# A six-stage fp32 transformer kernel on one core: norm weights of two units applied in the split, rotary angles earlier, a shorter wait of the up units, square sums behind the first pair

## The reference, cut to what matters

```python
def sq_relu_mlp(hn, w1, w2):                  # mlp0, mlp1; w1 1024x4096, w2 4096x1024
    return jnp.square(jax.nn.relu(hn @ w1)) @ w2

# mla: h is the residual stream, normed twice with different weights
ckv = rmsnorm(h, src_g) @ w_kv_a              # 1024 x 320: 256 latent + 64 rotary columns
cq  = rmsnorm(rmsnorm(h, norm_mix_g) @ w_q_a, q_g)   # w_q_a 1024 x 384
ang = positions[..., None] * inv_freq         # rotary angles; cos(ang), sin(ang) turn k_pe and q_pe
h   = h + attention(...) @ w_o
h   = h + sq_relu_mlp(rmsnorm(h, norm_mlp_g), w1, w2)
```

## Time and profile before

| | |
|---|---|
| median of three runs | 1063.13 us |
| profiled execution | 1063.45 us, span 1061.6 us |
| PE (matmul) busy | 1005.8 us, 95% of the span |
| DVE busy | 632.8 us, 60% |
| ACT busy | 484.3 us, 46% |
| POOL busy | 62.2 us, 6% |
| chain that ended last | PE 84%, DVE 8%, ACT 4%, issue 2% |
| mean granted TensorE clock | 0.974 |

### The profile page before, as it was taken

The page is one execution under the profiler, slowest core; times in us unless marked ns, Lnnn a source line. Parts: engine busy times, 40 slices in busy tenths (PEclk is TensorE's granted clock), DMA queues, the critical chain, the costliest instruction groups (busy, mean ns, idle before and its releaser), DMA issues.

```text
span 1061.6 us, 16624 instructions
## 1 busy us (share of the span) xinstructions
PE 1005.8 (95%) x6867; PEld 934.8 (88%) x6867; DVE 632.8 (60%) x748; ACT 484.3 (46%) x619; POOL 62.2 (6%) x63
## 2 busy tenths in 40 slices
PE   7989889889999999898999999999799999999997
PEld 7988778779999999898998899999699988999996
DVE  4377654467676676667555755555765755545554
ACT  5447522156455455542444544344445644444442
POOL 1000232020000000001000000000400000000000
PEclk9989979999999999999999999999999999999999
DMA  9733400046555555353555565556446236655640
GB/s 295 200 117 120 159 1 1 1 140 222 176 196 185 174 194 160 125 166 121 185 178 179 172 197 175 186 194 191 125 137 181 93 107 218 196 187 173 195 159 40
DMA packets 128591, 165.12 MB, mean 156 GB/s; under 512 B 20862, under 2 KB 111419, under 8 KB 128411
## 3 DMA queue, kind: packets, MB, share of 16 engines
q1 hardware_dynamic: 127067, 159.57, 46.8%
q0 software_dynamic: 1312, 4.74, 1.5%
q10 hardware_dynamic: 160, 0.07, 0.0%
HBM read 163.32 MB, written 1.05 MB: 155 GB/s over the span
## 4 chain that ended last, share of the span: by engine, by line
PE 84%; DVE 8%; ACT 4%; issue 2%; POOL 1%; DMA 0%; POOLq 0%; DVEq 0%; ACTq 0%
PE ps L224 26%; PE ps L225 25%; PE ps L226 25%; DVE w_lo L205 1%; ACT w_hi L197 1%; PE ps L990 1%; PE ps L1716 1%; PE ps L1710 1%; ACT act_tmp L339 1%; PE ps L1721 1%; DVE act_lo L649 1%; PE ps L1011 1%; PE ps L891 1%; ACT act_tmp L1040 1%; DVE union L1983 0%
## 5 line engine op out<-in xcount | busy, mean ns | idle before, releaser
L205 DVE TENSOR_TENSOR w_lo<-raw,w_hi 128x2048 fp32r<-128x2048 f32 (+1 forms) x152 | 343.3, 2263 | 167.8 <-ACT w_hi L197 166.8
L224 PE MATMUL ps<-hT_hi,w_hi 128*128 128x256 f32 x1192 | 341.2, 286 | 6.0 <-ACT act_tmp L623 3.7
L225 PE MATMUL ps<-hT_hi,w_lo 128*128 128x256 f32 x1192 | 339.2, 285 | 0.0
L226 PE MATMUL ps<-hT_lo,w_hi 128*128 128x256 f32 x1192 | 339.0, 284 | 0.0
L197 ACT ACTIVATE w_hi<-raw 128x2048 fp32r<-128x2048 f32 (+1 forms) x152 | 287.1, 1891 | 101.9 <-PE ps L226 93.8
L224 PEld LDWEIGHTS ps<-hT_hi,w_hi 128*128 128x128 f32 x1192 | 230.5, 193 | 8.9 <-issue 4.5
L225 PEld LDWEIGHTS ps<-hT_hi,w_lo 128*128 128x128 f32 x1192 | 230.6, 193 | 1.7
L226 PEld LDWEIGHTS ps<-hT_lo,w_hi 128*128 128x128 f32 x1192 | 230.6, 193 | 0.0
L224 PE MATMUL ps<-w_hi,act_hi 128*128 128x512 f32 x416 | 163.9, 394 | 5.5 <-DVE act_lo L649 5.5
L225 PE MATMUL ps<-w_hi,act_lo 128*128 128x512 f32 x416 | 163.4, 393 | 0.0
L226 PE MATMUL ps<-w_lo,act_hi 128*128 128x512 f32 x416 | 162.8, 391 | 0.0
(11 more groups left out here) (289 smaller groups left out, 945.9 us busy)
## 6 DMA issues: line engine op xcount, KB each, us to landing
raw<-in_mlp_w_dram SPq DMA_DIRECT2D x64, 1024.0 KB, 5.3
raw<-in_w_up_dram SPq DMA_DIRECT2D x22, 1024.0 KB, 5.0
raw<-in_a_w_in_dram SPq DMA_DIRECT2D x16, 1024.0 KB, 5.4
raw<-in_w_in_dram SPq DMA_DIRECT2D x12, 1024.0 KB, 5.8
raw<-in_w_down_dram SPq DMA_DIRECT2D x11, 1024.0 KB, 5.0
raw<-in_a_w_out_dram SPq DMA_DIRECT2D x8, 1024.0 KB, 4.9
raw<-in_w_out_dram SPq DMA_DIRECT2D x4, 1024.0 KB, 5.0
raw<-in_b_w_o_dram SPq DMA_DIRECT2D x4, 1024.0 KB, 5.0
```

The source lines that it names most:

```text
L205: nc.vector.tensor_tensor(w_lo[:, s, 0:n], raw[:, r, 0:n], w_hi[:, s, 0:n].bitcast(F32), ALU.subtract).then_inc(lo_ready, 1)
L224: nc.tensor.matmul(o, a[0], b[0], start=start, stop=False, skip_group_check=shared)
L225: nc.tensor.matmul(o, a[1], b[0], start=False, stop=False, skip_group_check=shared)
L226: return nc.tensor.matmul(o, a[0], b[1], start=False, stop=stop, skip_group_check=shared)
```

## The change

Five edits:

1. Of the three `mla` units, POOL multiplies only u0. For u0+1 and u0+2 the split itself applies the weights: `split_hi` is a row of ACT multiplications with a per-row weight, `split_lo` a row of DVE scalar_tensor_tensor operations (raw times weight minus w_hi), one for each of the 8 row blocks and each column range: 8 pieces of 256 columns for u0+1, 16 pieces of 128 columns for u0+2.
2. `mla_loads` is issued before POOL's norm of `mlp0` instead of behind it, and the five operations of pair 14 in the angle chain move to pair 1 (cuts 6 and 11). Sine and cosine stay at pair 14.
3. up(j) waits for the activation of pair j-2 instead of pair j-1, and up(1) for none.
4. In `mlp0` and `mlp1` the square sums (`sums_act`, `sums_dve`) come behind pair 0 instead of ahead of it.
5. `at_lo` of the third attention group comes before the split of the last w_o unit instead of behind it.

```diff
-            gained = {u0: [(0, UC, G_SRC)], u0 + 1: [(0, UC, G_MIX2 + 8)],
-                      u0 + 2: [(0, P, G_MIX2 + 8), (P, UC, G_SRC)]}
+            early_gain = u0
+            gained = {u0 + 1: [(0, UC, G_MIX2 + 8)], u0 + 2: [(0, P, G_MIX2 + 8), (P, UC, G_SRC)]}
...
+            if u == early_gain:
+                act.wait_ge(gain_in, 1)
             if u in gained:
-                act.wait_ge(gain_in, list(gained).index(u) + 1)
-            nc.scalar.activation(w_hi[:, s, 0:n], raw[:, r, 0:n], ACT.Copy).then_inc(hi_ready, 1)
+                for c, at in pieces(u):
+                    mul = nc.scalar.mul(w_hi[:, s, at], raw[:, r, at], c)
+                mul.then_inc(hi_ready, 1)
+            else:
+                nc.scalar.activation(w_hi[:, s, 0:n], raw[:, r, 0:n], ACT.Copy).then_inc(hi_ready, 1)
...
-            nc.vector.tensor_tensor(w_lo[:, s, 0:n], raw[:, r, 0:n], w_hi[:, s, 0:n].bitcast(F32),
-                                    ALU.subtract).then_inc(lo_ready, 1)
...
+            if u in gained:
+                for c, at in pieces(u):
+                    sub = nc.vector.scalar_tensor_tensor(w_lo[:, s, at], raw[:, r, at], c, w_hi[:, s, at].bitcast(F32),
+                                                         ALU.mult, ALU.subtract)
+                sub.then_inc(lo_ready, 1)
+            else:
+                nc.vector.tensor_tensor(w_lo[:, s, 0:n], raw[:, r, 0:n], w_hi[:, s, 0:n].bitcast(F32),
+                                        ALU.subtract).then_inc(lo_ready, 1)
...
+        def pieces(u):
+
+            return [(par[:, g + k:g + k + 1], slice(k * UC + c0, k * UC + c1)) for k in range(KT) for c0, c1, g in gained[u]]
...
         def plain_pe(pe, f, per, n):
             def step(j, m, u, i):
                 pe.wait_ge(lo_ready, u + 1 + i * PERIOD)
-                pe.wait_ge(f.t, f.base + j)
+                if not (isinstance(j, int) and j == 1):
+                    pe.wait_ge(f.t, f.base + j - 1)
                 up(W[m], u)
...
             step(0, 0, f.u0, 0)
+            if n in UNSCALED:
+                sums_act(act, n)
             each_pair(act, f, per, step, lambda j: f.u0 + 2 * j - 1)
...
             step(0, 0, f.u0, 0)
+            if n in UNSCALED:
+                sums_dve(dve, n)
             each_pair(dve, f, per, step, lambda j: f.u0 + 2 * j - 1)
...
-            for u in gained:
-                gain_pool(pool, u)
+            gain_pool(pool)
             norm_pool(pool, n)
...
-            cuts = {0: (0, 6), 1: (6, 12), mpairs - 2: (12, 17)}
+            cuts = {0: (0, 6), 1: (6, 17)}
...
+            at_lo(dve, gs[2])
             split_lo(dve, u0 + 12)
-            at_lo(dve, gs[2])
             at_lo(dve, gs[3])
...
+                if "mla" in stages[n + 1:n + 2]:
+                    mla_loads(pool, n + 1)
                 if st not in ("mix", "mla"):
                     norm_pool(pool, n, mone if n in UNSCALED else None)
...
-                if "mla" in stages[n + 1:n + 2]:
-                    mla_loads(pool, n + 1)
```

More of the change, by code:

```diff
@@ L204, in split_lo, with gain_pool @@
             dve.wait_ge(hi_ready, u + 1 + PERIOD * i)
-            nc.vector.tensor_tensor(w_lo[:, s, 0:n], raw[:, r, 0:n], w_hi[:, s, 0:n].bitcast(F32),
-                                    ALU.subtract).then_inc(lo_ready, 1)
-        def gain_pool(pool, u):
+            if u in gained:
[8 more added lines that the diff above has]
+            return [(par[:, g + k:g + k + 1], slice(k * UC + c0, k * UC + c1)) for k in range(KT) for c0, c1, g in gained[u]]
+        def gain_pool(pool):
+            u = early_gain
             pool.wait_ge(landed[u % RAW], landed_at[u])
             v = raw[:, u % RAW, 0:UNIT].rearrange("p (k n) -> p k n", k=KT)
[L212 to L215, removed]
+            nc.gpsimd.tensor_tensor(v, v, par[:, G_SRC:G_SRC + KT].unsqueeze(2).to_broadcast([P, KT, UC]),
+                                    ALU.mult).then_inc(gain_in, 1)
         def weights(u, k):
@@ L615, in plain_pe, with plain_act @@
                 down(u, (tiles2(act_hi, m), tiles2(act_lo, m)), last=True)
-        def plain_act(act, f, per, func, extra=None):
+        def plain_act(act, f, per, func, n, extra=None):
             def step(j, m, u, i):
@@ L635, in plain_act, with plain_dve @@
             step(0, 0, f.u0, 0)
+            if n in UNSCALED:
+                sums_act(act, n)
             each_pair(act, f, per, step, lambda j: f.u0 + 2 * j - 1)
-        def plain_dve(dve, f, per, factor, extra=None):
+        def plain_dve(dve, f, per, factor, n, extra=None):
             def step(j, m, u, i):
@@ L903, in gmlp_act @@
                 split_hi(act, u0 + j + 3)
-            plain_act(act, f, 3, ACT.Gelu)
+            plain_act(act, f, 3, ACT.Gelu, n)
         def gmlp_dve(dve, n, f):
@@ L934, in gmlp_dve @@
             dve.wait_ge(s_cp, GT)
-            plain_dve(dve, f, 3, lambda j, m: svT[:, bass.ds(j * 2, 2) if not isinstance(j, int) else slice(2 * j, 2 * j + 2), :].rearrange("p t s -> p (t s)"))
+            plain_dve(dve, f, 3, lambda j, m: svT[:, bass.ds(j * 2, 2) if not isinstance(j, int) else slice(2 * j, 2 * j + 2), :].rearrange("p t s -> p (t s)"), n)
         a_s, a_b, a_c, a_nm, a_e = sem("a_s"), sem("a_b"), sem("a_c"), sem("a_nm"), sem("a_e")
@@ L2087, in _ @@
                     split_hi(act, first_unit[st] + SPL - 1)
-                    sums_act(act, n)
+                    if st == "mla":
+                        sums_act(act, n)
                 else:
@@ L2106, in _ @@
                 elif "mla" in stages[n + 1:n + 2]:
-                    plain_act(act, passes[st], 3, ACT.Relu, angles_act)
+                    plain_act(act, passes[st], 3, ACT.Relu, n, angles_act)
                 else:
-                    plain_act(act, passes[st], 3, ACT.Relu)
+                    plain_act(act, passes[st], 3, ACT.Relu, n)
                 if st in posts:
@@ L2125, in _ @@
                         split_lo(dve, first_unit[st] + u)
-                    if n in UNSCALED:
+                    if st == "mla":
                         sums_dve(dve, n)
@@ L2139, in _ @@
                 elif "mla" in stages[n + 1:n + 2]:
-                    plain_dve(dve, passes[st], 3, lambda j, m: act_tmp[:, m, :], angles_dve)
+                    plain_dve(dve, passes[st], 3, lambda j, m: act_tmp[:, m, :], n, angles_dve)
                 else:
-                    plain_dve(dve, passes[st], 3, lambda j, m: act_tmp[:, m, :])
+                    plain_dve(dve, passes[st], 3, lambda j, m: act_tmp[:, m, :], n)
                 if st in posts:
```

2 lines of the change are left out of this document (1 added, 1 removed).

## The result

The changed kernel took 1050.99 us (median of 4 runs, 1049.72 to 1051.64), the kernel before, run beside it, 1062.93 us (1062.10 to 1063.21): 11.9 us between the medians. The ratio of the runs is 0.9882, 95% interval 0.9862 to 0.9902, so the change makes the kernel 1.2% faster. The forecast was 1048.0, with 1046.0 to 1052.5 as its range. The profiled execution took 1051.26 us with a span of 1049.5; its mean granted clock is 0.979, before 0.974.

What follows compares the result with a forecast made beforehand. PE, busy 95% of the span, bounds the kernel, so only its waits and low clock can be gained. 7.0 + 8.3 - 0.6 + 0.4 = 15.1 us off 1063.45 gives 1048.3, as median 1048.0; range 1046.0 to 1052.5.

Steps and rivals of the forecast that it cites:

- Starts of mlp0 and mlp1, 7.0 us: At up(1) of both passes: the 1.84 us wait and 1.7 us of lost clock go, 3.5 us each.
- the wait returns at down(0): Rival at both starts: act_lo 0.8 us or more late, clock falls, each gains 1.0 instead of 3.5; 1053, chance 0.13.
- End of mlp0, 8.3 us: Last down unit of mlp0: the 5.5 us wait for act_lo and 2.8 us of low clock behind it go.
- Start of mla, -0.6 us: At up(u0+1): PE waits 0.6 us for DVE's eight pieces, no low clock counted; bounds 0 and 1.9.
- the factor, for which I kept 0.7 us in the bound: In mla: POOL's factor for the latent may come at most 0.7 us later than PE asks; none counted.
- Attention, +0.4 us: In the attention: at_lo ahead of the split lets PE go on earlier, gain 0.4 us, bounds 0 and 1.0.
- Angles, nothing: Early loads and five angle operations in pair 1: worth nothing by themselves, cost nothing; 2.4 us without cover.
- The sum, 15.1 us: Whole kernel: 7.0 + 8.3 - 0.6 + 0.4 us off the profiled execution's 1063.45.
- As summed, within 2 us: Likeliest case for the whole kernel: all terms go as summed, within 2 us; chance 0.68.
- pieces that stop PE long enough for the clock: Rival at the start of mla: 1.9 us of wait plus 1.7 of low clock, 3.6 instead of 0.6; 1051.0, chance 0.12.
- The stall at the end of `mlp0`: Rival: that stall stays in part, 1048.7, or the 8.3 us stay wholly, 1056.3; chance 0.04.
- pieces that would make the kernel slower: Rival in mla: the 24 DVE pieces take about 0.94 us each or more; at 1.1 each 1067, chance 0.02.

Runs made afterwards that it cites:

- old_wait: Changed kernel with up(j) again waiting for the activation of pair j-1, squares still behind pair 0; 1052.66 us, ratio 0.9873 to the kernel before.
- sums_ahead: Changed kernel with the square sums of mlp0 and mlp1 ahead of pair 0 again; 1051.10 us, ratio 0.9874 to the kernel before.
- all_pieces: Changed kernel with pieces for the first mla unit too, nothing multiplied on POOL; 1050.97 us, ratio 0.9865 to the kernel before.
- late_angles: Changed kernel with the last five angle operations back at pair 14, loads still early; 1048.81 us, ratio 0.9867 to the kernel before.
- no_pieces: Changed kernel with POOL multiplying all three mla units again, angles still early; 1054.88 us, ratio 0.9923 to the kernel before.
- no_atlo: Changed kernel with the third at_lo behind the split of the last w_o unit again; 1050.39 us, ratio 0.9865 to the kernel before.
- The second trace: Trace of the changed kernel run once more without edits; 1050.34 us (6 runs), ratio 0.9886 to the kernel before, mlp0 begun at 580.79 us.

## Why the prediction was right, and where its sum was off

**Starts of mlp0 and mlp1, 7.0 us: 6.96 measured.** The wait of 1.84 us and the lost clock both went, and down(0) got act_lo in time. The lost clock was less than the 1.7 us of the sum: up(1) took 7.31 us before and takes 5.85 now, 1.5 us; the rest of the gain is what a stop costs beyond its wait. act_lo came 5.5 us behind the start of up(1), as forecast; it was not within 0.1 us of being asked for but 0.3 ahead, for up(1) takes 5.85 us and not 5.6. That without edit 4 "down(0) would wait for 596.94, 0.8 us" holds: 0.66 us of wait, 0.97 and 0.93 a pass. The rival that the wait returns at down(0) is thus real as a mechanism, and edit 4 excludes it; its price was too high, though. It assumed that the clock is lost behind a wait of 0.8 us as well, and in both old_wait and sums_ahead the clock kept its level. A part of the good match is luck: in the gMLP the clock fell behind a wait of 2.36 us in six traces and not in two, so the low clock behind a wait of 1.84 us, which the sum counts as a gain, may not be certain either. It was there in both passes of both traces of before.

**End of mlp0, 8.3 us: 8.43 measured.** The reading of the long DVE operations as POOL's holds (act_lo of pair 14 in all_pieces, 4.10 to 0.69 us; L1352, 3.83 us before and 0.41 in late_angles). The prediction gave one sum for edits 1 and 2. The runs part them: the pieces alone give 8.1 (late_angles), the early angles alone 4.5 (no_pieces), both 8.4, so they mostly remove the same stall and don't add up. With what each costs or leaves in `mla` it is about 7.4, 3.3 and 7.7 us. The forecast of 2.7 us to spare was 2.6.

**Start of mla, -0.6 us: -0.72 measured** (-0.31 in the stage, with the 0.41 of edit 5 in it). Of this 0.44 is the wait for the pieces, forecast 0.6; from the norm's first hT_hi to up(u0+1) it is 8.72 us against 8.14, 0.58 in all. The small matmuls L1189 start 5.86 us after that, 5.76 before. From the first group of L1181 behind them to the second, which needs the latent's factor, it is 3.40 us, before 3.41, so the factor, for which I kept 0.7 us in the bound, costs nothing. The pieces took 3.24, 4.29 and, on ACT, 4.80 us; forecast 3.2, 4.2 and 4.6. The estimates from the Trainium skill's figures (VectorE: DVE Perf Modes, "The TRN2 errata — SBUF-src ops pay a fixed extra latency per instruction"; for DVE its formula for a single fp32 tensor_tensor) were 3.4 us for the eight and 4.7 for ACT's sixteen. The traces are nearer to these on ACT and farther on DVE, where a piece in a row takes 0.405 us and one in the mean of the earlier trace rows 0.476.

**Attention, +0.4 us: 0.41 measured** (no_atlo). The wait shrank from 1.03 to 0.62 us.

**Angles, nothing: nothing found on their own.** Their loads and the five operations in pair 1 cost no stage anything. To put the loads late again with edit 4 in place wasn't tried: DVE's angle operations in pair 0 would wait for loads that POOL issues behind the norm's sums, and DVE makes those sums only after pair 0, so by the order of the program the kernel would stop for good.

**The sum, 15.1 us: 15.1 by stages, 11.9 in the medians.** No step in the stages that the change touches failed. The forecast time is 3.0 us too low because the changed kernel loses time ahead of anything that the change touches: the two profiled executions differ by 12.2 us, and the changed kernel's is 2.91 us late at the start of `mlp0`. What the prediction mis-sized is how far executions differ there: for it the range kept the 1.0 us by which three runs lay below their median, while the 15 runs of the kernel before beside the first experiments spread from 1060.72 to 1067.72. "As summed, within 2 us", its likeliest case, is what the stages show; the median lies outside of it, and inside the range by some luck. It lies at the very number of a rival, 1051.0 for pieces that stop PE long enough for the clock. The traces refute that rival all the same, which the median alone could not.

Whether all of the 3 us is chance stays open. The second trace is 1.44 us early at `mlp0`, and the mean of the ten changed kernels about 1.6 us late against the mean of two of before; at 105 us none of the ten is ahead of either of the two, though two are within 0.1 us. Taking each kernel's ratio with its own difference by stages, the ratio for the change comes out at about 0.987, 13.9 us. The kernel before was run anew beside three groups of kernels; the four kernels beside the first (15 runs) give 13.0 us, the five beside the other two (13 and 11 runs) 14.9, and the first result 12.5. Whether the 1.2 us left are chance in a few executions, or a lasting effect of other code on how the first stages fall, these runs don't settle: two traces of before are too few.

**The other rivals.** The pieces cost 0.72 us and not 3.6, and the clock stayed (1.00 from 775 to 789 us). The stall at the end of `mlp0` didn't stay, and pieces that would make the kernel slower would have had to take 0.94 us each; they take 0.27 and 0.41.

## What to carry to other kernels

A wait of the bounding engine is priced with the clock behind it: shortening two waits of 1.84 us to 0.8 brought 2.5 us each, ending them the last 0.9. That price is not certain: one wait of 2.36 us cost the clock in some executions and not in others. When operations of one engine take several times their usual length, look at which other engine ends at the same moment; moving two multiplications from POOL into operations that ACT and DVE do anyway paid 8.1 us for 0.7. And with changes of 1%, compare stages between common marks in the traces, since here they agree to 0.1 us where the stages ahead of the first changed line differed by up to 5.7.

## What the runs showed of the hardware that was not expected

- PE's waits of 0.66, 0.78 and 1.03 us, in the midst of full work, left the granted clock at 1.00. One of 1.84 us was followed by 0.50 (from 593 to 596 us in the first trace of before), in both passes of both traces of before.
- The same wait of 2.36 us in the gMLP was followed by a low clock in six traces (0.66 in the mean of 5 us) and by 1.00 in two, at a difference of 1.6 us. The length of the wait alone doesn't tell.
- One program differs between executions in its first stages, where PE often waits, by steps of up to 1.7 us: the fourth weight unit was split from 27.88 or 28.25 us on in the two traces of before, and the dips of the clock moved.
- A DVE tensor_scalar of 128x256 with a single SBUF input took 1.98 us beside POOL's multiplication, 0.35 without it (no_pieces, L1381 and all_pieces, L1391).
